# A dilated attention layer whose sum over groups is split by halves of heads

## What is computed

```python
u = rmsnorm(h, norm_pre[0])
# three groups g with dilation 1, 4, 16; 16 heads of 64 channels in each
# o[g], m[g], l[g]: unnormalised values, row maximum and denominator of softmax per head
# out = sum over g of o[g] * exp(m[g] - max_g m) / sum over g of l[g] * exp(m[g] - max_g m)
y = out * silu(gate)                    # gate = u @ w_in[:, 9 * D:]
h = h + rmsnorm(y @ w_out, norm_post[0])
```

## Time and profile before

| | |
|---|---|
| median of 3 runs | 2489.29 us (2485.29 to 2494.46) |
| profiled execution | 2492.45 us |
| its span | 2490.6 us |
| TensorE busy | 2196.4 us, 88% |
| VectorE, ScalarE, POOL busy | 954.9, 877.5, 862.7 us |
| mean granted TensorE clock | 0.941 |
| the dilated layer's mixing lies at | 683 to 731 us of the span |
| its output projection ends at | 776 us |

### The profile page before, as it was taken

One profiled execution on the slowest core, in us unless ns is written; L12 is line 12 of the kernel. 1 busy time (PEld: TensorE's weight loads), 2 busy tenths in 40 slices (PEclk: granted clock), 3 DMA queues, 4 the chain that ended last, 5 costly groups with the idle time before them and its releaser, 6 DMA issues. The chain is left out here.

```text
span 2490.6 us, 26029 instructions
## 1 busy us (share of the span) xinstructions
PE 2196.4 (88%) x10048; PEld 1737.8 (70%) x10048; DVE 954.9 (38%) x1603; ACT 877.5 (35%) x1756; POOL 862.7 (35%) x454
## 2 busy tenths in 40 slices
PE   4999999999937998757999999897987998999998
PEld 3877788888836776546677877675675456887876
DVE  1333334634443356553253321237553652110111
ACT  2544445655353554423232222232322222322231
POOL 3322233333313422243344344342224323443442
PEclk9999999999968999978999999898998998999999
DMA  4312122222322321222342233232223332332321
GB/s 159 95 51 69 52 80 74 86 86 83 129 89 64 100 68 51 72 75 93 108 144 93 85 77 102 65 93 85 77 77 129 125 115 63 102 102 85 99 90 66
DMA packets 130634, 221.32 MB, mean 89 GB/s; under 512 B 8744, under 2 KB 58456, under 8 KB 130304
## 3 DMA queue, kind: packets, MB, share of 16 engines
q1 hardware_dynamic: 110720, 168.63, 22.2%
q0 software_dynamic: 9104, 32.66, 4.0%
q10 hardware_dynamic: 10688, 18.35, 2.1%
HBM read 199.40 MB, written 19.62 MB: 88 GB/s over the span
## 5 line engine op out<-in xcount | busy, mean ns | idle before, releaser
L2236 POOL TENSOR_TENSOR lo_ring<-raw_ring,hi_ring 128x1024 fp32r<-128x1024 f32 (+1 forms) x304 | 729.9, 2423 | 1194.9 <-ACT hi_ring L1889 1194.8
L853 PE MATMUL bank<-xh,hi_ring 128*128 128x512 f32 x1472 | 601.6, 409 | 5.3 <-DVE xl L1335 3.3
L853 PE MATMUL bank<-xh,lo_ring 128*128 128x512 f32 x1472 | 582.7, 396 | 0.0
L853 PE MATMUL bank<-xl,hi_ring 128*128 128x512 f32 x1472 | 582.2, 395 | 0.0
L1889 ACT CAST hi_ring<-raw_ring 128x1024 fp32r<-128x1024 f32 (+1 forms) x304 | 303.4, 1045 | 516.2 <-PE bank L853 495.2
L853 PEld LDWEIGHTS bank<-xh,hi_ring 128*128 128x128 f32 x1472 | 282.7, 192 | 77.3 <-issue 18.3
L853 PEld LDWEIGHTS bank<-xh,lo_ring 128*128 128x128 f32 x1472 | 281.6, 191 | 61.7
L853 PEld LDWEIGHTS bank<-xl,hi_ring 128*128 128x128 f32 x1472 | 282.5, 192 | 58.1 <-issue 2.6
L853 PE MATMUL bank<-hi_ring,xh 128*128 128x512 f32 (+1 forms) x608 | 249.8, 411 | 11.2 <-POOL lo_ring L2236 6.4
L853 PE MATMUL bank<-lo_ring,xh 128*128 128x512 f32 (+1 forms) x608 | 241.8, 398 | 0.0
L853 PE MATMUL bank<-hi_ring,xl 128*128 128x512 f32 (+1 forms) x608 | 241.7, 397 | 0.0
(11 more groups left out here) (246 smaller groups left out, 2483.4 us busy)
## 6 DMA issues: line engine op xcount, KB each, us to landing
raw_ring<-in_ffn_w_in SPq DMA_DIRECT2D x176, 256.0 KB, 3.1
raw_ring<-in_dil_w_in SPq DMA_DIRECT2D x80, 512.0 KB, 3.7
raw_ring<-in_ffn_w_out SPq DMA_DIRECT2D x44, 512.0 KB, 3.8
raw_ring<-in_diff_w_in SPq DMA_DIRECT2D x32, 512.0 KB, 3.7
raw_ring<-in_w_in SPq DMA_DIRECT2D x32, 512.0 KB, 3.6
arena<-scratch_heads POOLq DMA_DIRECT2D x4, 1584.0 KB, 13.9
scratch_gates<-arena ACTq DMA_DIRECT2D x24, 256.0 KB, 2.0
arena<-scratch_gates POOLq DMA_DIRECT2D x24, 256.0 KB, 4.1
```

The source lines that it names most:

```text
L853: ins = T.matmul(bank[pb][:, 0:S if p.form == "feature" else p.cols], lhsT, rhs, start=(k == 0 and m == 0), stop=(k == p.K - 1 and m == le ...
L2236: G.tensor_tensor(lo, raw_ring[:, p % RAW, 0:q.kq * q.n], hi.bitcast(F32), ALU.subtract).then_inc(lowered, 1)
```

## The change

Heads are split in halves of 8. The data of each tile and half have their own place in `arena`, their own load and their own semaphore.

- The attention of unit 4 is interleaved at 1.1 advances a job in place of 0.85.
- The first half (heads 0 to 7, units 0, 2, 4) is loaded and mixed beside the attention of unit 5, at fixed jobs of the gate panels (`first_half`): two tiles loaded ahead, the next two behind the sums of the first two. Per tile and half VectorE scales 12 head slices and ScalarE 12 (`SCALED` = 4). The gate product of the first half stands at gate jobs 10, 11, 14 and 15.
- `last_store` puts the row `post0` and the four loads of the second half right behind the store of unit 5; the first tile's ratio, weights and scaling of the second half stand at the last two gate jobs.
- Behind the gate panels the four half tiles are turned into banks 4 to 7 (`mix_turn`), rounded and lowered (`mix_lower`). The first output projection panel then runs its first four jobs, which need the first half only. Behind them each tile's second half gets its gate product, turn, rounding and lowering, followed by one job of the panel's last step, which waits for it (`late`).
- Between these stand the scaling, ratio, sum and weights of the next tiles. The barrier at the start of `finish_layer` is gone for this layer; `finish_layer` runs only the second panel and what follows. The row lies at the end of `arena`.

```diff
-UNIT_RATIO, GATE_RATIO, FIRST_HEADS = 0.85, 2.5, 14
+UNIT_RATIO, LAST_RATIO, GATE_RATIO = 0.85, 1.1, 2.5
...
-def finish_layer(plan, w, row_name, next_name):
-    plan.job("over", False)
-    plan.job("row", row_name)
-    for c in range(2):
+def finish_layer(plan, w, row_name, next_name, first=0):
+    if first == 0:
+        plan.job("over", False)
+        plan.job("row", row_name)
+    for c in range(first, 2):
...
-        interleave(projections(u), side, UNIT_RATIO)
+        interleave(projections(u), side, LAST_RATIO if u == 5 else UNIT_RATIO)
         side = attention(u)
-    def first_heads():
-        plan.job("mix_load")
-        for _ in range(FIRST_HEADS):
+    def first_half():
+
+        for n in range(2):
+            plan.job("mix_load", 0, n)
+        for step in range(16):
             yield
-        plan.job("mix_ratio", 0)
-        plan.job("mix_weight", 0)
-        plan.job("mix_scale", 0)
-
-    interleave(gate_panels(plan, w, 9 * D, 0), chain(side, first_heads()), GATE_RATIO)
+            if step % 3 == 2 and step < 12:
+                plan.job("mix_ratio", 0, step // 3)
+            elif step % 3 == 0 and 0 < step < 13:
+                n = step // 3 - 1
+                plan.job("mix_weight", 0, n)
+                plan.job("mix_scale", 0, n)
+            elif step % 3 == 1 and 1 < step < 14:
+                n = step // 3 - 1
+                plan.job("mix_sum", 0, n)
+                if n + 2 < NT:
+                    plan.job("mix_load", 0, n + 2)
+            if step in (9, 10, 13, 14):
+                plan.job("mix_gate", 0, (9, 10, 13, 14).index(step))
+            if step == 14:
+                plan.job("mix_ratio", 1, 0)
+            if step == 15:
+                plan.job("mix_weight", 1, 0)
+                plan.job("mix_scale", 1, 0)
+
+    def last_store():
+        plan.job("row", "post0")
+        for n in range(NT):
+            plan.job("mix_load", 1, n)
+        yield
+
+    side, beside = chain(side, last_store()), first_half()
+    owed = 0.0
+    next(beside)
+    for _ in gate_panels(plan, w, 9 * D, 0):
+        owed += GATE_RATIO
+        while owed >= 1.0:
+            owed -= 1.0
+            next(side, None)
+        next(beside, None)
+    run_all(side)
+
+    use = [plan.job("mix_turn", 0, n, banks=(4 + n,)) for n in range(NT)]
+    plan.job("mix_ratio", 1, 1)
+    plan.job("mix_sum", 1, 0)
+    plan.job("mix_weight", 1, 1)
     for n in range(NT):
+        plan.job("mix_lower", 0, n)
+    plan.parts = tuple(((f"drained{4 + n}", use[n][0]),) for n in range(NT))
+    late = [(), (), (), ()]
+    main = plan.panel("y", "dil_w_out", 0, 512, "tile", at=(0,), late=late)
+    for _ in range(4):
+        next(main)
+    for n in range(NT):
+        plan.job("mix_gate", 1, n)
+        use = plan.job("mix_turn", 1, n, banks=(4 + n,))
+        late[n] = ((f"drained{4 + n}", use[0]),)
         if n + 1 < NT:
-            plan.job("mix_ratio", n + 1)
-        plan.job("mix_sum", n)
-        if n + 1 < NT:
-            plan.job("mix_weight", n + 1)
-        plan.tile_parts("mix", n)
-        if n + 1 < NT:
-            plan.job("mix_scale", n + 1)
-        plan.job("lower", n)
+            plan.job("mix_scale", 1, n + 1)
+            if n + 2 < NT:
+                plan.job("mix_ratio", 1, n + 2)
+            plan.job("mix_sum", 1, n + 1)
+            if n + 2 < NT:
+                plan.job("mix_weight", 1, n + 2)
+        plan.job("mix_lower", 1, n)
+        next(main)
+    run_all(main)
+    plan.parts = ((), (), (), ())
...
+                else:
+                    for name_value in p.late[b]:
...
+                elif kind == "mix_turn":
+                    half, n = a
                     T.wait_ge(mixed, job.n + 1)
-                    turn_tile(job, mix[:, a[0] % 2, :], a[0])
+                    empty(4 + n, job.use[0])
+                    for k in range(4):
+                        ins = T.transpose(tile(bank[4 + n], k), tile(mix[half][n], k), ident)
+                    ins.then_inc(filled[4 + n], 1)
...
+                    if p.w == "dil_w_out":
+                        V.wait_ge(mixed, NT + o + 1)
...
+            def mix_sum(m, half, n):
+                H = heads_of(half, n)
+                o_ = mix[half][n].rearrange("p (h r) -> p h r", h=8)
+                V.wait_ge(heads_scaled, 2 * m + 2)
+                V.wait_ge(slices_scaled, m + 1)
+                if half == 0 and n == 0:
+                    V.wait_ge(stored[0], 16 * (1 + 1 + 4))
+                V.tensor_tensor(o_, H[:, 0, :, 0:HD], H[:, 1, :, 0:HD], ALU.add).then_inc(v_step, own.up())
                 V.wait_ge(v_step, own.n)
-                V.tensor_tensor(m, m, H[:, 2, :, 0:HD], ALU.add).then_inc(heads_mixed, 1)
-
-            def mix_tile(n):
-                V.wait_ge(heads_mixed, n + 1)
-                V.wait_ge(drained[n], gate_panel[0, 1].use[n])
-                V.scalar_tensor_tensor(mix[:, n % 2, :], mix[:, n % 2, :], 0.5, mix_gate[n], ALU.mult, ALU.mult).then_inc(mixed, 1)
+                V.tensor_tensor(o_, o_, H[:, 2, :, 0:HD], ALU.add).then_inc(heads_mixed, 1)
+
+            def mix_gate_half(m, half, n):
+                V.wait_ge(heads_mixed, m + 1)
+                V.wait_ge(drained[n], gate_panel[0, half].use[n])
+                V.scalar_tensor_tensor(mix[half][n], mix[half][n], 0.5, tile_gate(n, half), ALU.mult, ALU.mult).then_inc(mixed, 1)
+
+            def mix_lower(half, n):
+                b, cols = 4 + n, slice(n * P, (n + 1) * P)
+                tiles_rounded.up()
+                V.wait_ge(x_rounded, tiles_rounded.n)
+                V.tensor_tensor(xl[:, 4 * half:4 * half + 4, cols], bank[b][:, :].rearrange("p (a b) -> p a b", a=4),
+                                xh[:, 4 * half:4 * half + 4, cols].bitcast(F32), ALU.subtract).then_inc(drained[b], 1)
...
+                    A.wait_ge(weights_made, job.n + 1)
+                    for g, h in [(1, h) for h in range(SCALED, 8)] + [(2, h) for h in range(8)]:
+                        o_ = heads[half][n][:, g, h * ROW:h * ROW + HD]
+                        ins = A.activation(o_, o_, ACT.Copy, scale=corr[job.n % 2][:, 8 * g + h:8 * g + h + 1])
+                    ins.then_inc(slices_scaled, 1)
+                elif kind == "mix_turn":
+                    half, n = a
+                    A.wait_ge(filled[4 + n], job.use[0])
+                    A.copy(xh[:, 4 * half:4 * half + 4, n * P:(n + 1) * P], bank[4 + n][:, :].rearrange("p (a b) -> p a b", a=4)).then_inc(x_rounded, tiles_rounded.up())
...
+                    if half == 0:
+                        G.wait_ge(stored[0], 16 * (1 + 1 + 4))
+                        G.wait_ge(stored[1], 16 * (1 + 1))
+                        if n == 0:
+                            G.wait_ge(filled[6], use_of["v_turn", plan.count["v_turn"] - 1][0])
+                        elif n >= 2:
+                            G.wait_ge(heads_mixed, n - 1)
+                    elif n == 0:
+                        G.wait_ge(stored[1], 16 * (1 + 1 + 4))
+                    src = scratch[:, n * P:(n + 1) * P, half * HALF_ROW:(half + 1) * HALF_ROW]
+                    G.dma_start(heads[half][n], src.rearrange("g p c -> p g c")).then_inc(heads_landed[half][n], 16)
```

115 lines of the change are left out of this document (53 added, 62 removed).

## The result

The changed kernel took **2501.60 us** (median of 7 runs, 2495.79 to 2505.46), the kernel before 2489.29 (7 runs, 2483.93 to 2494.46). The comparison of the two on record gives a ratio of 1.0039, 95% interval 1.0022 to 1.0056; the two medians are 1.0049 apart. That is slower by 0.2 to 0.6%, with the 12.3 us between the medians just inside the half per cent that the text called no change, but with the other sign than the forecast, 14.6 us above the 2487 and 1.6 above the end of the range. The profiled execution took 2504.15 us (span 2502.3) against 2492.45 (span 2490.6).

What follows compares the result with a forecast made beforehand. TensorE bounds the kernel except for 47.5 us of mixing it waits for; terms from gate end to projection end summed to 89.8 us against 92.1, 2.3 less, so 2487 us as a median, range 2473 to 2500.

Steps and rivals of the forecast that it cites:

- The prices: Durations of the new half-size mixing operations, each bounded by its full-size row and half of it; gate product 0.65 us.
- part 4: Output projection: four first-half steps 10.9, cold start 2.8, waits 20.7, four late steps 10.9, low clock 3.5, last panel 21.8 us.
- Part 1: Unit 4's attention ends four steps earlier, TensorE runs the same instructions: cost 0, between -0.4 and +1.0 us.
- Part 2, waits: First-half mixing beside the gate panels delays unit 5's attention, turn 5 and values 7: +5.5 us, 2 to 8.
- Part 2, clock: Clock may fall after the wait at values 7 beside the gate panels: +1.8 us, 0 to 3.0.
- Part 2, POOL: POOL's queue of loads, lowerings and last store beside the gate panels: second-half data arrive just in time, cost 0.
- Part 3: Gate end to first projection step, a chain of second-half mixing and first-half roundings: 11.9 us, between 10 and 14.
- Four steps and cold start: First four output projection steps, over the first half: 10.9 us plus 2.8 for a cold clock.
- The steps and the last panel: Four single projection steps behind turns, 10.9 us, plus 3.5 for low clock (0 to 8.1), and last panel 21.8.
- C: Clock stays at 0.50 from the first projection step through the turns into the last panel: 2505 us, chance 0.10.
- the likeliest case: Most matmuls put beside the mixing are paid back in stalls and half-size chains: 2487 us, 2478 to 2497, chance 0.65.
- the wait before a turned step exceeds 9 us: Sign that would prove the forecast wrong, in the output projection; longest wait priced there was 8.1 us.

Runs made afterwards that it cites:

- hold2: Changed kernel plus 5 matmuls of constants, in a bank already free, at two TensorE waits beside unit 5's attention: 2501.5 us.
- memset: Changed kernel with POOL zeroing the low part of the dilated layer's gate and output projection weights instead of subtracting: 2492.4 us.
- early_lock: early with POOL zeroing the low parts of the gate and output projection weights instead of subtracting: 2468.1 us.
- fill: Changed kernel plus 16 matmuls of constants in TensorE's waits around the second half's turns: 2487.8 us.
- early: Changed kernel with one first-half projection step ahead of each second-half turn, the last twelve steps unbroken behind: 2473.1 us, 2476.7 when repeated.
- whole: Changed kernel with all four second halves turned first, then all 16 projection steps run unbroken: 2486.7 us.
- ratio85: Changed kernel with unit 4's attention back at the old share of 0.85 instead of 1.1: 2504.4 us.
- hold: Changed kernel plus 9 matmuls of constants at two TensorE waits beside unit 5's attention, in banks the waiting job overwrites: 2505.8 us.
- order: Changed kernel with the second half's first weights, scaling, ratio and sum placed behind the first half's four roundings: 2494.4 us.

## Why the prediction was wrong

The text named the end of the projection as its instant: forecast 2.3 us earlier, measured 7.5 later, **9.8 us** apart. Another 4.2 us of the profiled execution lie behind the stretch (1715.1 against 1710.9), in code that the change leaves alone. Two steps of the text failed. The prices took VectorE's durations as if no other engine ran beside it, so the collision with POOL stood at nothing; and in part 4 the clock's share of the single steps was put at 3.5 us and came to about 8.9 (the last four single steps and the last panel took 41.6 us, where full clock makes 32.7). In its own steps:

- **Part 1 (cost 0, up to +1.0): right.** The stretch's start came 0.87 us later, which is within scatter (it lies between 613.6 and 619.2 in the twenty profiles, at 617.10 and 619.08 in the other two of the kernel before), and undoing the part changed nothing that can be told.
- **Part 2, waits (+5.5): mechanism right, size too high.** ScalarE did just what was written out: scalings, two casts, gate activation, and only then the exponentials of score 5; the turn waited 1.66 us, not 2.1, and the last values 2.98, not 4.6.
- **Part 2, clock (+1.8): too low.** I priced one fall. There were two, after 1.66 us and after 2.98, at 0.50 for 6.8 and 3.4 us. About 4.8 us were lost: the gate panels end 74.7 us behind the stretch's start instead of 66.4, and 3.5 of these 8.3 us are waits. The row that I took for the bound was of a wait of 2.78 us, and I let a wait shorter than that pass as harmless. `hold2` shows 2.5 us for the first. Gate end at 692.75 for a forecast near 691: 1.9 us, made up of 0.9 of the start, -2.0 of the waits and +3.0 of the clock.
- **Part 2, POOL (cost 0, "just hidden"): right for what it priced, blind for what counted.** The loads came in time; no step waited for one. But POOL's subtractions now lay beside VectorE's mixing, and I asked only what stands behind them in POOL's queue, never what they do to the engine beside them.
- **The prices: the first step that failed.** Each new operation was "bounded by its full-size row and by half of it", which took the durations from a stage in which POOL was idle. 1.03 us became 7.19, 0.18 became 4.85, 0.69 became 2.92. Being bounded from both sides by rows of the same engine in the same stage doesn't bound what another engine does to it in a new one. `memset` shows this at 3.6 to 6.3 us of the stretch, `early_lock` at 7 to 10 in the better order.
- **Part 3 (11.9, 10 to 14): 14.3, outside.** The order was as written, and the third turn, which I had let lie inside, waited 3.04 us for a sum that stood behind the scaling held until 694.08; the last gate product came late with it. +2.4.
- **Part 4.** Four steps and cold start 13.7: 12.6 (707.04 to 719.68), -1.1. Waits of 3.3, 8.1, 5.1 and 4.2: 2.9, 9.5, 5.2 and 4.3. The one that grew is the one in which scaling, at 728.78, met a subtraction: +1.4 there, -0.2 in the others together. The steps and the last panel, 36.2: 41.6, **+5.4**, the largest term and the second step that failed. Three of the four steps behind turns (735.05, 745.75, 755.51) ran at 1.2 GHz; I had taken 3.5 of a possible 8.1 for it. `fill` shows 5.4 to 8.1 us for the clock.

1.9 + 2.4 - 1.1 + 1.4 - 0.2 + 5.4 is the 9.8. The clock's shares and the collision's overlap in it, since a longer wait also lengthens the time at low clock, and the two experiments aren't to be added.

Of the rivals, none came as written. C needs all eight early steps at 1.2 GHz; the first four ran at it only until 710.5, and the last panel from 762 on at full clock. But its mechanism did weigh more than in the likeliest case, and the page that I cited there ("TensorE: Matmul & The Clock Gate", section "HAM oscillation — how this bites in real kernels", of the Trainium skill), by which the clock's 3.5 us would be 8.1 and the change cost 2.3 us, was the better guide: `early` and `whole`, which keep steps together, are both faster than the changed kernel. Of the marks in the last part, "the wait before a turned step exceeds 9 us" is the one that came: 9.5.

**What stays open.** The totals differ by 12.3 us, the end of the projection by 7.5 and, in a second profile, by less (stretches 4.1 us apart). Behind the stretch the changed kernel's profiles have 1715.1 and 1714.1 us, those of the kernel before 1710.9, 1704.1 and 1714.1; the eight profiles of kernels that keep the four steps ahead of the turns (these two, ratio85, hold, hold2, memset, order, fill) average 1713.0, from 1702.4 to 1718.5, against 1709.7 for the three. So some us of the median's difference may lie in code that isn't changed, and that the result lies outside the range, by 1.6 us, is within this scatter (the second profile's execution took 2498.66 us); that the stretch is longer than before in both profiles, and not shorter, is outside the 0.2 us by which it repeats there. As to the part behind the stretch, with a scatter of 10 us in one kernel it can't be told from chance, and no run here says what sets it.

## What to carry to other kernels

Before work of one engine is moved beside another's, look for every pair of engines that will now run together and never did, and look in the whole trace for how each stretches the other: here a row of 1.76 beside one of 0.68 us was there to be read. When waits can't be avoided, put the ready work between them so that the last of it runs unbroken: one step ahead of each turn and twelve behind won 12 to 15 us of the stretch where four, then one behind each turn, lost 4 to 7. And matmuls of constants in the waits tell what the clock costs, but by themselves they are no cure: here they brought 5.4 to 8.1 us in one order and nothing in another.

## What the runs showed of the hardware

- VectorE's operations on two operands in SBUF stand still beside POOL's subtraction of 128x1024 pieces: 0.18 us to 4.85, 1.03 to 7.19, whatever their own size. Two subtractions in a row (4.75 us) held such an operation through both at 672.38, let one in between them at 710.41 (2.43 us), and at 728.15 VectorE's operation took 0.70 us, no longer than alone, and the pair of subtractions 5.10. Beside POOL's memset of the same size they are not stretched.
- The granted clock fell from 1.00 to 0.50 at 652.49, when TensorE was at work again (651.18) behind a wait of only 1.66 us, and stayed there for 6.8 us; behind a wait of 2.98 us it fell at 669.55 and stayed there for 3.4 us. The length of the wait alone doesn't tell the price.
- VectorE's held operation can begin before the subtraction's own row does. The 7.19 us from 686.89 are two scalings, of which the second, of 256 columns, begins at 687.50 and takes 6.58; the subtraction begins at 689.06, while POOL issues the loads from 686.04. It isn't the issuing that holds: in `memset` L1472 takes 1.03 us at 687.37, beside the issue of 685.94 to 689.00. Whether POOL's subtraction begins earlier than its row says, no run here shows.
- Which of two neighbouring operations is caught by such a collision differs between executions of one program, and moved this stage by 2.8 us (2.99 and 5.78 us of wait, stretches of 147.5 and 150.3).
